# Attention of a hybrid decoder layer written out as one sequence of 192 blocks, with two sets of query and key buffers, and its borders to the projection and inside the gate and up products rewritten

## The reference

```python
for window, dilation in ((128, 1), (512, 4), (2048, 16)):
    o, lse = dilated_pattern(q, k, v, window, dilation)
    outs.append(o); lses.append(lse)
w = jax.nn.softmax(jnp.stack(lses, axis=0), axis=0)
out = jnp.sum(w[..., None] * jnp.stack(outs, axis=0), axis=0)
```

## Time and profile before

| | us |
|---|---|
| median of 3 runs | 2645.27 |
| lowest and highest | 2637.58, 2646.13 |
| the profiled execution | 2636.76 |
| its span | 2635.0 |
| busy: PE, PEld | 2504.8, 2105.8 |
| busy: DVE, ACT, POOL | 1270.7, 884.8, 612.4 |

### The profile page before, as it was taken

The page is one execution under the profiler, slowest core; times in us unless marked ns, Lnnn a source line. Parts: engine busy times, 40 slices in busy tenths (PEclk is TensorE's granted clock), DMA queues, the critical chain, the costliest instruction groups (busy, mean ns, idle before and its releaser), DMA issues.

```text
span 2635.0 us, 36209 instructions
## 1 busy us (share of the span) xinstructions
PE 2504.8 (95%) x12312; PEld 2105.8 (80%) x12312; DVE 1270.7 (48%) x2460; ACT 884.8 (34%) x1762; POOL 612.4 (23%) x389
## 2 busy tenths in 40 slices
PE   8999999978989979998899999889999999999998
PEld 6888888878988857777688888678888878888887
DVE  4322456524544567777766656766566632101011
ACT  4301122236766723233544444434444421000000
POOL 0198555431343156664000000000000000000000
PEclk9999999988977979999999999999999999999999
DMA  5411223377458145555333333343333246424242
GB/s 182 139 51 60 72 100 119 126 188 172 118 124 222 53 151 164 164 166 195 127 122 105 101 117 108 116 148 104 115 109 118 92 150 210 167 100 159 94 163 105
DMA packets 259214, 342.10 MB, mean 130 GB/s; under 512 B 18208, under 2 KB 162208, under 8 KB 258848
## 3 DMA queue, kind: packets, MB, share of 16 engines
q1 hardware_dynamic: 259104, 340.67, 40.9%
HBM read 222.76 MB, written 117.83 MB: 129 GB/s over the span
## 4 chain that ended last, share of the span: by engine, by line
PE 54%; DVE 3%; issue 3%; POOL 3%; ACT 1%; DMA 0%; SPq 0%; POOLq 0%; DVEq 0%; ACTq 0%
PE fin_psum_bank L1630 31%; PE fin_psum_bank L1706 17%; PE fin_psum_bank L1190 4%; POOL mx_parts L1359 1%; DVE ff_b_lo L1920 1%; PE fin_psum_bank L1158 1%; POOL mx_q_heads L1337 1%; POOL mx_stat L1346 0%; PE fin_psum_bank L1154 0%; PE fin_psum_bank L1166 0%; POOL mx_ssq L1039 0%; DVE ff_total L2101 0%; DVE w_out L1008 0%; PE fin_psum_bank L1177 0%; POOL mx_parts L1362 0%
## 5 line engine op out<-in xcount | busy, mean ns | idle before, releaser
L1630 PE MATMUL fin_psum_bank<-ff_b_hi,ff_w_hi 128*128 128x512 f32 x1232 | 485.2, 394 | 26.3 <-DVE ff_b_lo L1920 13.4
L1630 PE MATMUL fin_psum_bank<-ff_b_lo,ff_w_hi 128*128 128x512 f32 x1232 | 483.0, 392 | 0.0
L1630 PE MATMUL fin_psum_bank<-ff_b_hi,ff_w_lo 128*128 128x512 f32 x1232 | 482.7, 392 | 0.0
L1706 PE MATMUL fin_psum_bank<-ff_down_hi,ff_acts 128*128 128x512 f32 x1408 | 436.6, 391 | 7.0 <-DVE ff_down_lo L2088 4.5
L1706 PEld LDWEIGHTS fin_psum_bank<-ff_down_hi,ff_acts 128*128 128x128 f32 x1408 | 265.3, 188 | 64.7 <-issue 4.9
L1630 PEld LDWEIGHTS fin_psum_bank<-ff_b_hi,ff_w_hi 128*128 128x128 f32 x1232 | 233.7, 190 | 79.3 <-DVE ff_b_lo L1920 15.5
L1706 PE MATMUL fin_psum_bank<-ff_down_lo,ff_acts 128*128 128x512 f32 x704 | 274.7, 390 | 0.0
L1630 PEld LDWEIGHTS fin_psum_bank<-ff_b_hi,ff_w_lo 128*128 128x128 f32 x1232 | 233.5, 190 | 49.0
L1630 PEld LDWEIGHTS fin_psum_bank<-ff_b_lo,ff_w_hi 128*128 128x128 f32 x1232 | 234.0, 190 | 48.3
L1912 POOL TENSOR_TENSOR ff_ssq<-ff_ssq,ff_minus_half 128x1 f32<-128x1 f32 x16 | 8.8, 550 | 926.6 <-DVE ff_ssq L2092 926.6
L1916 DVE TENSOR_TENSOR ff_w_lo<-ff_raw,ff_w_hi 128x512 fp32r<-128x512 f32 x176 | 124.2, 707 | 158.9 <-ACT ff_w_hi L1737 158.9
(11 more groups left out here) (179 smaller groups left out, 4331.2 us busy)
## 6 DMA issues: line engine op xcount, KB each, us to landing
ff_raw<-in_w_gate SPq DMA_DIRECT2D x22, 1024.0 KB, 6.4
ff_raw<-in_w_up SPq DMA_DIRECT2D x22, 1024.0 KB, 5.4
a_hi<-ff_a_hi SPq DMA_DIRECT2D x88, 256.0 KB, 2.1
a_lo<-ff_a_lo SPq DMA_DIRECT2D x88, 256.0 KB, 2.3
ff_acts<-a_hi SPq DMA_DIRECT2D x88, 256.0 KB, 2.8
ff_acts<-a_lo SPq DMA_DIRECT2D x88, 256.0 KB, 3.1
att_out<-at_orow SPq DMA_DIRECT2D x192, 66.0 KB, 2.0
mx_att_in<-att_out SPq DMA_DIRECT2D x16, 792.0 KB, 4.8
```

The lines of the kernel that those rows point to most:

```text
L1630: last = nc.tensor.matmul(to, w[:, i, k, :], b[i][:, k, :], start=fresh and k == 0 and which == 0, stop=k == KH - 1 and which == 2, skip_g ...
L1706: last = nc.tensor.matmul(bank[:, ORDER[b], :], acts[n % 4][:, part, c * P:(c + 1) * P], w[k][:, half * GROUP:(half + 1) * GROUP], start=k ...
```

## The change

Attention: the loops of PE, DVE and ACT are gone; each issues one sequence of 192 blocks, n = 0 to 191. PE at n issues scores of n+4, the turn of n+1 and values of n-1. The turned weights have three PSUM banks and three `probT` buffers, `orow` is a ring of 16. There are two sets of `q_near` and `k_near` (`first["near"][s]`), and the loads of the next unit are spread over the blocks j with j % 7 in (0, 2, 4, 5), from block 0 of a unit on. `w_out` is loaded in four parts in the last unit. For space, `w_out` and buffers of later stages trade places (`MOVED`).

Projection: the 12 value loads of the first unit are issued after the last retention value is stored, before the 8 pairs. Of the 24 query and key loads, 10 are issued before the last pair's stores, 10 between its first four stores, and 4 (`LATE`) right behind the fourth.

Gate and up products: the loads of the first two tiles of the second half, the difference (now on DVE, in a buffer of its own, `b_diff`), the first two sums and the rounding of P1 and P2 move from between the halves into the last turns of the first half; `low_b` of P4 and P3 and three `low_a` move into the first turn of the second.

```diff
@@ load_qk, at the end of project, SP @@
...
+                sp.wait_ge(group_done, VALUES)
+                for r in range(NR):
+                    sp.wait_ge(row_free[r], 16 * (CHUNKS // NR) + 16)
+                for n in range(VALUE_LOADS):
+                    load_values(sp, D, first, 0, n)
+                def between(pos, i):
+
+                    if i < GROUPS:
+                        n = QK_DMAS + 3 * i
+                        for n in range(n, min(n + 3, 2 * QK_DMAS - 2)):
+                            load_qk(sp, D, first, 0, 0, n)
+                    if i == GROUPS - 1:
+                        sp.wait_ge(group_done, VALUES + 8 * pos + GROUPS)
+                        for n in LATE:
+                            load_qk(sp, D, first, 0, 0, n)
...
+                for n in range(QK_DMAS - 2):
+                    load_qk(sp, D, first, 0, 0, n)
+                body(end - 1, None)
@@ attention, SP @@
...
+                def unit(u, s, more=True):
+
+                    sp.wait_ge(permuted, BY_16 * u + C_PERMUTED)
+                    sp.sem_inc(waited, 1)
+                    sp.wait_ge(scored, NB * u + C_SCORED)
+                    sp.sem_inc(waited, 1)
+                    n = 0
                     for j in range(NB):
-                        if more and j == NEAR:
-
-                            sp.wait_ge(scored, NB * u + NEAR + C_SCORED)
-                            sp.wait_ge(permuted_k, 4 * u + 4)
-                            sp.wait_ge(permuted_4, 2 * u + 2)
-                            sp.wait_ge(permuted_16, 2 * u + 2)
                         store(u, j)
-                        if more and NEAR <= j < NEAR + 2 * QK_DMAS:
-                            load_qk(sp, D, first, u + 1, j - NEAR)
+                        if more and j % 7 in (0, 2, 4, 5) and n < 2 * QK_DMAS:
+                            load_qk(sp, D, first, u + 1, 1 - s, n)
+                            n += 1
                         if more and j and j % 4 == 0:
                             load_values(sp, D, first, u + 1, j // 4 - 1)
+                        if not more and j % 10 == 2 and j < 40:
...
@@ attention, PE @@
...
-                with pe.Fori(0, NU // 2) as it:
-                    def at(J):
-                        return 2 * it + J // NB, J // NB, J % NB
-
-                    for J in range(AHEAD):
-                        u, _, j = at(J)
-                        scores(u, j)
-                    turn(2 * it, 0)
-                    for J in range(2 * NB):
-                        u, s, j = at(J)
-                        if j == NB - 1:
-                            values(u, j)
-                        if J + AHEAD < 2 * NB:
-                            un, _, jn = at(J + AHEAD)
-                            scores(un, jn)
-                        if J + 1 < 2 * NB:
-                            un, _, jn = at(J + 1)
-                            turn(un, jn)
-                        if j < NB - 1:
-                            values(u, j)
+                for n in range(AHEAD):
+                    scores(n)
+                turn(0)
+                for n in range(ALL):
+                    if n + AHEAD < ALL:
+                        scores(n + AHEAD)
+                    if n + 1 < ALL:
+                        turn(n + 1)
+                    if n:
+                        values(n - 1)
+                values(ALL - 1)
@@ attention, ACT @@
...
+                for n in range(ALL):
+                    act.wait_ge(maxed, n + 1)
+                    for h in range(2):
+                        pr = prob[:, n % 4, h, keys[n % NB]]
+                        last = nc.scalar.activation(pr, pr, ACT.Exp, bias=orow[:, n % RING, 2 * OW + h:2 * OW + h + 1], scale=-1.0)
+                    last.then_inc(exped, 1)
+                    if n >= 2 and n % 2 == 1:
+                        copy_turned(n - 2)
+                    if n >= 4:
+                        copy_out(n - 4)
+                copy_turned(ALL - 1)
+                for n in range(ALL - 4, ALL):
+                    copy_out(n)
@@ ffn, ACT, between the halves @@
-                high_b(act, P1, 1)
-                high_a(n, C22)
-                high_b(act, P2, 1)
                 high_b(act, P6, 1)
                 high_b(act, P5, 1)
+                high_b(act, P7, 1)
+                high_a(n, C22)
+                high_b(act, P4, 1)
                 high_a(n, C21)
-                high_b(act, P7, 1)
-                high_b(act, P4, 1)
+                high_b(act, P3, 1)
                 high_a(n, C12)
-                high_b(act, P3, 1)
@@ ffn, DVE @@
...
+            if closing:
+                first_sum(dve, 1)
+                low_b(dve, P1, 1)
+                second_sum(dve, 1)
             if not last:
-                for i in (P6, P5, P7):
+                for i in (P6, P5) if closing else (P6, P5, P7):
...
-                first_sum(dve, 1)
-                low_b(dve, P1, 1)
-                second_sum(dve, 1)
-                direct(n)
                 third_sum(dve, 1)
                 low_b(dve, P2, 1)
+                direct(n)
                 low_b(dve, P6, 1)
+                low(dve, P7, n + 1, 0)
+                low_b(dve, P5, 1)
                 merge(n, 1, C12)
-                low_b(dve, P5, 1)
-                low_a(n - 1, C22)
-                low_a(n - 1, C21)
                 low_b(dve, P7, 1)
-                low_b(dve, P4, 1)
-                low_a(n - 1, C12)
-                low_b(dve, P3, 1)
```

311 lines of the change are left out of this document (161 added, 150 removed).

## The result

| | before | changed |
|---|---|---|
| median of four runs each, on the same chip | 2643.81 us | 2579.89 us |
| lowest and highest | 2637.58, 2646.13 | 2578.81, 2581.05 |
| profiled execution: time, span | 2636.8, 2635.0 | 2581.05, 2578.9 |
| mean granted clock | 0.970 | 0.985 |

The account below looks back on a forecast made before the run. PE, busy 95% of the span, was taken as the bound. Savings of 12 (projection), 41 (attention) and 13 (between halves) make 66: 2636.8 - 66 = 2571, put at 2574 for the median; range 2551 to 2600.

Parts of the forecast that it names:

- Step 1: End of the projection: without value loads between SP's last stores, PE starts attention at about 556.2, 12 us earlier.
- Step 2: Projection: the 12 value loads, issued after the values, hold SP at most 32 us under 44 us of cover: 0.
- Step 3: Attention: earlier loads and ring 16 remove DVE's 30.7 us of store waits, PE's 12.9 and 4.3, and idle before half clock.
- the clean price of 293: Attention without waits or half clock: four units from PE's block times, 289.5 us, plus 3.5 for filling and draining.
- The 36 us of clock: Attention before the change: 84 us at half clock, each doing 0.57 of the work, lose 36 us.
- Step 4: Attention's three seams: PE waits 4 us at each for POOL's casts before block 16, plus 1 us of clock: 15 us.
- the 300 to 312 that were to show the mechanism: Sign to look for: attention of 300 to 312 us at a mean clock of 0.95 or more.
- Step 5: Between the halves of gate and up products: DVE's earlier work lets P1 of turn 23 end at 1720.5: 13 us saved.
- Step 6: `w_out` in four parts and new buffer places: 0, since nothing waits for them before mix.
- POOL is in time: Rival, chance 0.22: last load lands within 3 us, so the 15 us at attention's seams fall away: 2559.
- The DMA engines stay the limit at the end of each unit: Rival, chance 0.20: half of attention's about 19 us lost per seam stays, 28 us instead of 15: 2587.
- The clock: Rival, chance 0.03: PE falls to 1.2 GHz over eight cycling banks without DMA stalls; attention wholly so gives 2780.

Follow-up runs that it names:

- old_values: Changed kernel with the first unit's value loads moved back to the end of the projection, as before the change: 2592.06 us, ratio 0.9806 to the kernel before.
- qk_dense: Changed kernel with a query or key load of the next unit behind every block from 0 to 23: 2563.07 us, ratio 0.9698 to the kernel before.
- ring8_late: Changed kernel with a ring of 8 for 16 and the next unit's loads behind each of blocks 16 to 39: 2607.61 us, ratio 0.9867 to before.
- ring8: Changed kernel with a ring of 8 rows for 16, loads still behind four blocks of seven: 2594.73 us, ratio 0.9822 to the kernel before.
- two_banks: Changed kernel with two banks and buffers of turned weights, values and copies of their sums one block earlier: 2579.65 us, ratio 0.9767 to before.
- gate_first: Changed kernel with turn 24's gate weights loaded ahead of turn 21's stores C22, C21 and C12 on SP: 2579.29 us, ratio 0.9751 to before.
- qk_by34: Changed kernel with the next unit's query and key loads behind two blocks of three, 0 to 34: 2564.28 us, ratio 0.9703 to before.
- qk_late: Changed kernel with the next unit's loads behind each of blocks 16 to 39, ring of 16 kept: 2600.19 us, ratio 0.9847 to before.
- dense_gate: Changed kernel with a query or key load behind every block from 0 and the gate load ahead of the stores: 2559.25 us, ratio 0.9676 to before.
- before_ring16: Kernel before the change with only the ring of 16 in place of 8: 2628.16 us, ratio 0.9935 to the kernel before.

## Why the prediction was right, and where its steps were off

The forecast was 2574 us (2551 to 2600) and 2579.89 came out; faster, as given 0.95. From profile to profile the sum was 66 us and 56 are there: 2571 forecast and 2581 measured, 10 us off. That the forecast is within 6 us of the median is in part luck: 3 us were added for the scatter of the kernel before, and the changed kernel's profile lies 1 over its median. The terms are better judged by the stages.

- **Step 1, -12: -12.6.** PE at 556.2 was forecast and 555.5 measured; in old_values PE starts 10.6 us later again. The number was right; of its two links, SP's issue time and ACT's late copies, old_values shows that the first is enough.
- **Step 2, 0: 0.** The projection's products are not delayed: the last copy stands at 553.98.
- **Step 3, the clean price of 293: shown.** qk_dense, with 1.1 us of waits on POOL and 0.4 on DVE, takes 293.2. The 36 us of clock were right too: PE is busy for 326.2 us before and for 291.4 in qk_dense, 34.8 less. The mechanism was half right. The step held DVE's waits for stores in the ring of 8 to be what stalls and slows PE, and did not count where the loads stand. Four kernels with the new code vary both. By the medians: with late loads the longer ring gives 7.4 us and the spread then 20.3; in the other order the spread gives 12.9 (ring8_late to ring8) and the ring 14.8 (by the ratios to before 5 and 23, 12 and 16). In the profiles attention goes 343.4, 332.4, 312.6 the one way and 343.4, 319.8, 312.6 the other. So each is worth much, and which is worth more hangs on the order. The ring alone, before the change, gives attention 9.7 us. The rest, 5.1 us from before to ring8_late between the profiles (some 10 more by the medians), would be the unrolled sequence with its third bank and the second set of buffers; no run took these apart, but for the third bank, which is worth nothing here (two_banks). 3.3 of it were the loop's start on PE, and DVE restarted its loop at each seam as well, which I had not looked at. The second set is what lets the loads stand this early.
- **Step 4, 15 us of waits and clock in all: about 21.** The last load landed 7.3 us after its issue (7), the casts took 23.4 us (23.6), the waits were 5.1, 2.9 and 5.5, a little over the 12 forecast. The miss in kind is the place of the wait: I looked for it only at block 16, behind POOL. The same late load ends the wait for keys at block 4, and that takes 8.4 of the 13.5 us. It changes what would help: a faster POOL could not have won more than the second half, an earlier load won all of it. The miss in size is the clock: PE is busy for 297.7 us where qk_dense needs 291.4, so 6.3 us went at half clock, where the step had 3. With that, attention came out at 312.6 and not 308, just over the 300 to 312 that were to show the mechanism.
- **Step 5, -13: -9.1.** P7 of turn 22 was put at 42 us behind P1 of turn 21 and stands 42.3 behind it (1668.30 - 1626.04); P1 of turn 23 ends 48.0 behind, 47.8 were forecast. The step ended there. It followed DVE and ACT into the second half, but not SP's queue, though the change moves the low parts of three stores' data behind DVE's sixth and seventh split, and the gate load stands behind those stores. This wait is worth 4.9 us (gate_first: 873.2 to 868.3): with it removed the gain is 14.0, and the step's 13 is met.
- **Step 6, 0: +1.8 in mix.** The prediction's own bound for this was 3. The longer drain of the pipeline accounts for 1.5 of it (6.46 to 7.94 us for mix's first load); the rest is inside the scatter of mix, 344.6 to 349.9 us over the kernels with the new code.
- **Rivals.** *POOL is in time* (2559) describes what a different spacing does: qk_by34 and qk_dense reached 2564 and 2563 by it. *The DMA engines stay the limit at the end of each unit* (2587) was the nearer picture of the cause, the changed kernel being between it and the forecast; qk_late, at 2600, is that case. *The clock*, with eight cycling banks, did not come: in dense_gate attention runs at a mean of 0.99 with them. The Trainium skill (TensorE: Matmul & The Clock Gate, A second HAM failure mode: psum-queue depth-cycling) has the clock going up and down for groups of matmuls that cycle through banks; by that rule these stretches would be slow, and the trace does not agree.

## What to carry to other kernels

When loads are prefetched into a second set of buffers, what counts is when the last of them lands: spread them so that the big ones are through long before the first instruction that reads them, and never pack them against the end, where a backlog adds to the place. A short ring of store buffers that waits was here a sign that the DMA engines were full; a longer ring alone turned PE's slow time into longer waits at the next reader, and gave 9.7 us of the 35.9 in attention. When work is moved forward on two engines, follow each queue that stands behind them, the DMA issuer's too, up to the first load that the next stage needs.

## What the hardware showed that I had not expected

- The half clock is not bound to full DMA engines. Before, the two came together. In the changed kernel the engines are as full (share 1.10, 265 GB/s) while PE keeps 1.00 and issues 91 matmuls in 10 us, the fast pace; what the slow stretch at the first seam has ahead of it is idle time of PE (2.73 us before 657.82), though the length of the wait alone does not tell: after 2.40 us before 634.11 the clock stayed at 1.00, after 1.78 before 714.03 it was 0.83 over 712 to 722:

```profile
620.00:630.00 10.00, 10.00 (x91) 10.00 (x90) 6.20 (x40) 8.66 (x31) 0.00 (x0) 1.00 1.10 265
655.00:660.00 5.00, 2.27 (x12) 2.18 (x11) 1.24 (x9) 1.28 (x4) 5.00 (x2) 0.70 0.15 40
660.00:665.00 5.00, 5.00 (x29) 5.00 (x29) 1.39 (x6) 1.90 (x6) 5.00 (x2) 0.62 0.14 41
```

- Half clock while PE was idle cost nothing here. In qk_late the 13 us around the first seam have a mean clock of 0.77 and only 4.43 us of PE work. Its attention of 0.94 would by the mean alone be 40 us at half clock and 17 us lost; PE's busy time tells what it was, 300.0 us for 291.4 in qk_dense, so 9. The granted clock has to be read together with busy time.

```profile
627.00:640.00 13.00, 4.43 (x40) 4.29 (x38) 3.81 (x23) 5.38 (x17) 0.00 (x0) 0.77 1.09 239
```

- A loop's restart was longer with full DMA engines: DVE 3.4 and 3.5 us at shares of 0.36 and 0.47 (before), 13.8 and 14.3 where the share was 1.09 to 1.14 for most of the time (before_ring16); PE 3.3 and 8.2 us in the same two traces. Each time the last packet of code starts a fixed time before the engine does, 2.3 us for DVE and 3.0 for PE.
- Issuing on SP was slower with a backlog at the DMA engines. In old_values the first four value loads took 2.10 us to issue (at 529.55), the last eight of the same size 19.64 (at 543.26, DMA share 1.06 over the 20 us). A load's price on its queue is not a constant, and mine for them, 2.6 each, was that of a backlog too.
- The kernel before scatters over 8.6 to 14 us in a group of runs, most of the changed ones over 2 to 7. Where stalls hang on a DMA backlog, one profile is a sample: the three seams of one execution of the changed kernel waited 5.1, 2.9 and 5.5 us.
